# Moving the matmul row buffers of a two-part transformer to byte 64 modulo 512 of a partition

## The chip, the cores and the metric

The kernel runs on one core of a Trainium2 chip. Its time is the device time of one execution in microseconds (us); the figure used is the median of three runs. A core has five engines that run side by side and meet only at semaphores: TensorE (PE in the profile; its weight loads are shown apart as PEld), VectorE (DVE), ScalarE (ACT), GpSimd (POOL) and SyncE (SP), which here only issues weight DMAs. Tiles live in SBUF, 128 partitions wide; a "byte" of a buffer below is its start address inside each partition. Matmul results go to PSUM, which has eight banks.

## The reference, cut to what matters

Two transformer blocks in turn, each of two layers, on 256 rows of 1024 columns in float32. Every layer has a mixer and a gated feed-forward part, and almost all of the work is products of normalised rows with weights:

```python
for l in range(DEPTH):                       # first block
    h = rms_norm(x, g_mix[l])
    proj = h @ w_in[l]                       # 1024 x 10052: attention, convolutions, gates
    ...                                      # four branches, each @ a 512 x 1024 weight
    x = x + merged @ w_merge[l]
    h2 = rms_norm(x, g_ffn[l])
    gt = causal_dwconv(h2 @ w_ffn_gate[l], ffn_conv_w[l])
    x = x + (jax.nn.silu(gt) * (h2 @ w_ffn_up[l])) @ w_ffn_down[l]
...                                          # second block: layer 0 compressed and selected attention,
x = x + mix                                  # layer 1 dilated attention
x = x + swiglu(rmsnorm(x, norm_ffn[layer]), ffn_w_up[layer], ffn_w_down[layer])
```

## The kernel before

Each float32 operand of a product is split into a rounded high part and the remainder, both of type float32r, and a product is three passes: high by high, high by low, low by high (`three_passes`, lines 467 to 469). So every row buffer comes in two parts: `hT` (high and low, 2 x 8 x 256 columns in the tile `h_place`), `mixer_rows`, `ffn_rows`, `blocks_rows`, `dilated_rows` (the raw, turned rows before their norm is known, made in `raw_T`, line 538), `query_rows`, `branch` and `hidden`. All except `hT` are placed over one large tile, `work`, at an element given by hand.

Weights come as a stream of 277 units, most of them 1024 rows by 256 columns (128 partitions by 2048 elements, 1 MiB). SP loads a unit into one of three raw slots (line 2738); it may do so when the remainder of the unit three before has been made. ScalarE makes the high part into one of four `whi` slots (`make_high`, L435); VectorE, or GpSimd for some units of the mixers, makes the remainder into one of three `wlo` slots (`make_low`, L443), which frees the raw slot. A unit is 48 passes on TensorE (24 with 512 columns). A matmul has a stationary operand, loaded first, and a moving one, streamed past it. Where the result is wanted turned, a piece of 128 weight columns is stationary and the rows move (`columns_product`); elsewhere 128 rows are stationary and the weights move. In the profile the names after the arrow stand in the order moving, stationary: `psum<-hT,whi` has hT moving.

The program is a row of stages, in each of which every engine runs a list written out by hand: setup; twice mixer, merge product, feed-forward up, feed-forward down; compressed attention, its output product, feed-forward up and down; dilated attention, output product, feed-forward up and down; final norm. The mixer takes 48 units, the first four from `mixer_rows`, all later ones that read rows from `hT` (as moving operand 26, as stationary 10, one of them narrow). `ffn_up_stage` (line 855) takes 22 units, gate and up in turn: the first four from `ffn_rows`, 18 from `hT`. Its loop over pairs c runs, on ScalarE: high part of the unit four ahead, SiLU (L905), high part of the next, high part of the result (L909); on VectorE: the gate's norm or copy, its short convolution in the first block (L946, L949), the low part of the result before (L969), the product (L963), then two remainders of weights (L443). `take_unit` (line 455) makes TensorE wait for the remainder of a unit.

Later the compressed attention reads `hT` as moving operand in 8 units and the dilated one in 3; `add_rows_product` takes `hT` as stationary operand against 512 weight columns.

Of the kernel before, what the change touches and what calls it, by code (L numbers as in the profile page):

```python
# [28 lines left out]
P = 128  # L29
D = 1024  # L30
S = 256
TT = S // P
KT = D // P
# [200 lines left out]
def two_part_transformer(nc, a, consts, onehots, out):  # L234
    ctx = ExitStack()
    with ctx:
        place = {}

        def sb(name, shape, dt=F32):
            place[name] = -(-nc.sbuf_base // 32) * 32  # L240
            return ctx.enter_context(nc.sbuf_tensor(name, shape, dt))
# [2 lines left out]
            return Signal(ctx.enter_context(nc.semaphore(name)))  # L244

        x = sb("x", [P, TT, D])
        h_place = sb("h_place", [P, 2 * KT * S])
        raw = sb("raw", [P, RAW_SLOTS, UNIT])
        whi = sb("whi", [P, HIGH_SLOTS, UNIT], F32R)
        wlo = sb("wlo", [P, LOW_SLOTS, UNIT], F32R)  # L250
# [14 lines left out]
        at_h, at_work = place["h_place"], place["work"]  # L265

        def over(name, base, start, shape, dt=F32R):

            return nc.alloc_sbuf_tensor_at(name, [P] + shape, dt, offset=base + 4 * start)

        hT_both = over("hT", at_h, 0, [2, KT, S])
        hT = [hT_both[:, i] for i in range(2)]

        ROWS = 32
# [261 lines left out]
            root_ready.close(n)  # L536

        raw_T = {}
        for kind, rows_at in (("mixer", 19088), ("ffn", 14400), ("blocks", 15456), ("dilated", 17920)):
            raw_T[kind] = [over(f"{kind}_rows{i}", at_work, rows_at + i * KT * S, [KT, S]) for i in range(2)]  # L540
        part_sum = stat[:, 152:156]
        root = stat[:, 4:4 + TT]
# [2264 lines left out]
```

How the kernel before makes its waits and increments, by code:

```python
        def begin(eng):  # L393
            if stage[0]:
                eng.wait_ge(stage_done.sem, COMPUTE * stage[0])
# [1 line left out]
        def end(eng):  # L397
            eng.drain().then_inc(stage_done.sem, 1)
# [10 lines left out]
        def v_wait(n):  # L409
            nc.vector.wait_ge(vector_step.sem, n)
# [9 lines left out]
        def s_wait(n):  # L420
            nc.scalar.wait_ge(scalar_step.sem, n)
# [6 lines left out]
        def make_high(act, upto):  # L428
            while stream.high < min(upto, len(stream.units)):
                n = stream.high
                act.wait_ge(raw_landed[n % RAW_SLOTS], 16 * (n // RAW_SLOTS + 1))
                if n >= HIGH_SLOTS:
                    act.wait_ge(*stream.freed[n - HIGH_SLOTS])
                act.activation(part(whi, n, HIGH_SLOTS), part(raw, n, RAW_SLOTS), ACT.Copy).then_inc(high_made, 1)
                stream.high += 1
# [1 line left out]
        def make_low(eng, n):  # L438
            eng.wait_ge(high_made, n + 1)
            if n >= LOW_SLOTS:
                eng.wait_ge(*stream.freed[n - LOW_SLOTS])
            eng.tensor_tensor(part(wlo, n, LOW_SLOTS), part(raw, n, RAW_SLOTS),
                              part(whi, n, HIGH_SLOTS).bitcast(F32), ALU.subtract).then_inc(stream.low[n][0], 1)
# [10 lines left out]
        def take_unit(pe, n):  # L455
            pe.wait_ge(*stream.low[n])
            _, kt, _, _ = stream.units[n]
            return [part(b, n, k).rearrange("p (k c) -> p k c", k=kt) for b, k in ((whi, HIGH_SLOTS), (wlo, LOW_SLOTS))]
# [18 lines left out]
        def await_pair(pe):  # L478
            if handed_over:
                pe.wait_ge(*handed_over.pop(0))
```

## Time and profile before

| | us |
|---|---|
| median of three runs | 1822.07 |
| the three runs | 1816.26, 1822.07, 1826.09 |
| span of the profiled execution, first to last instruction | 1816.4 |
| TensorE busy, matmul | 1761.0 (97%) |
| TensorE busy, weight loads | 1663.7 (92%) |
| VectorE busy | 1220.7 (67%) |
| ScalarE busy | 932.6 (51%) |
| GpSimd busy | 124.6 (7%) |
| chain that ended last: TensorE's share | 84% |

The span is what the profile gives of the profiled execution's own time; it lies inside the range of the three timed runs. TensorE takes a matmul before the one ahead has ended, so the duration of one is longer than the distance from start to start; both are used below, and they are named apart. The granted clock of TensorE is shown in tenths of 2.4 GHz, over 40 slices of the span; it has two levels, 2.4 and 1.2 GHz.

### The profile page before, as it was taken

To read this page: it belongs to the slowest core of one execution; us is meant where nothing else is said; L and a number is where in the kernel's file an instruction comes from. 1 tells how busy PE (TensorE), PEld (TensorE's weight loads), DVE (VectorE), ACT (ScalarE), POOL (GpSimd) and SP (SyncE) were. 2 spreads that over 40 slices of the span, in tenths; PEclk is the share of its full clock that TensorE was granted. 3 is DMA by queue.
4 is the path that set the end of the run, shared out by engine and by line. 5 is a ranking of instruction groups with operands and counts; after the bars stand their busy time and mean duration, and the time that the engine had idled before them with its cause. 6 is when DMAs were issued, how large, how long until landed. Compare 5 with 4: busy or idle time off the path is not lost.

```text
span 1816.4 us, 31727 instructions
## 1 busy us (share of the span) xinstructions
PE 1761.0 (97%) x13416; PEld 1663.7 (92%) x13416; DVE 1220.7 (67%) x1927; ACT 932.6 (51%) x1291; POOL 124.6 (7%) x35
## 2 busy tenths in 40 slices
PE   7999999999999999999999998889999999999998
PEld 6999999899989999999999898769998899889986
DVE  6984855787749877567877466977554655655553
ACT  5445655454435545664544355755443565654442
POOL 1620300000004603000000000000000000000000
PEclk9899999999999999999999999989999999999999
DMA  7684546445554544546455546314555476435551
GB/s 236 174 207 128 180 133 210 163 163 186 207 188 146 186 150 153 186 140 206 149 190 190 177 156 170 123 64 139 186 186 209 165 215 166 129 121 181 186 220 70
DMA packets 248637, 305.75 MB, mean 168 GB/s; under 512 B 9267, under 2 KB 223631, under 8 KB 248496
## 3 DMA queue, kind: packets, MB, share of 16 engines
q1 hardware_dynamic: 235959, 289.66, 48.6%
q10 hardware_dynamic: 12536, 14.06, 4.0%
q8 instruction: 106, 1.74, 0.4%
q14 instruction: 36, 0.29, 0.0%
HBM read 299.51 MB, written 4.19 MB: 167 GB/s over the span
## 4 chain that ended last, share of the span: by engine, by line
PE 84%; DVE 7%; DMA 4%; ACT 3%; issue 1%; DVEq 0%; POOL 0%; SPq 0%; ACTq 0%; POOLq 0%
PE psum L467 25%; PE psum L468 25%; PE psum L469 25%; DVE wlo L443 2%; DMA raw<-in_w_in 1%; DMA raw<-in_a_w_in 1%; PE psum L2477 1%; PE psum L2503 1%; DMA x<-in_x 1%; DMA raw<-in_b_w_q 1%; PE psum L2489 1%; ACT whi L435 0%; ACT work L2563 0%; DVE work L2292 0%; PE psum L1119 0%
## 5 line engine op out<-in xcount | busy, mean ns | idle before, releaser
L435 ACT ACTIVATE whi<-raw 128x2048 fp32r<-128x2048 f32 (+2 forms) x277 | 526.6, 1903 | 543.9 <-PE psum L469 183.5
L443 DVE TENSOR_TENSOR wlo<-raw,whi 128x2048 fp32r<-128x2048 f32 x249 | 563.4, 2281 | 191.8 <-PE psum L469 157.5
L467 PE MATMUL psum<-hT,whi 128*128 128x256 f32 x2160 | 615.4, 285 | 4.9 <-DVE wlo L443 2.5
L469 PE MATMUL psum<-hT,wlo 128*128 128x256 f32 x2160 | 612.4, 284 | 0.0
L468 PE MATMUL psum<-hT,whi 128*128 128x256 f32 x2160 | 612.3, 283 | 0.0
L467 PEld LDWEIGHTS psum<-hT,whi 128*128 128x128 f32 x2160 | 414.7, 192 | 6.2 <-DVE wlo L443 3.1
L468 PEld LDWEIGHTS psum<-hT,whi 128*128 128x128 f32 x2160 | 414.6, 192 | 0.2
L469 PEld LDWEIGHTS psum<-hT,wlo 128*128 128x128 f32 x2160 | 414.4, 192 | 0.0
L443 POOL TENSOR_TENSOR wlo<-raw,whi 128x2048 fp32r<-128x2048 f32 (+1 forms) x28 | 123.4, 4411 | 588.7 <-ACT whi L435 401.2
L467 PE MATMUL psum<-whi,hT 128*128 128x256 f32 (+2 forms) x448 | 143.7, 321 | 1.1 <-issue 0.8
L469 PE MATMUL psum<-whi,hT 128*128 128x256 f32 (+2 forms) x448 | 143.0, 319 | 0.0
L468 PE MATMUL psum<-wlo,hT 128*128 128x256 f32 (+2 forms) x448 | 143.0, 319 | 0.0
L467 PE MATMUL psum<-whi,hidden 128*128 128x512 f32 x352 | 138.1, 392 | 1.1 <-issue 1.1
L468 PE MATMUL psum<-wlo,hidden 128*128 128x512 f32 x352 | 138.0, 392 | 0.0
L469 PE MATMUL psum<-whi,hidden 128*128 128x512 f32 x352 | 137.5, 391 | 0.0
L963 DVE TENSOR_TENSOR work<-work,psum 128x512 f32<-128x512 f32 x44 | 30.2, 687 | 134.4 <-PE psum L469 63.0
L467 PEld LDWEIGHTS psum<-whi,hT 128*128 128x128 f32 x448 | 88.3, 197 | 8.2 <-issue 3.3
L1476 DVE SCALAR_TENSOR_TENSOR psum<-work,par,psum 128x256 f32<-128x256 f32 x240 | 94.7, 480 | 0.1
L469 PEld LDWEIGHTS psum<-whi,hT 128*128 128x128 f32 x448 | 88.4, 197 | 5.0
L468 PEld LDWEIGHTS psum<-wlo,hT 128*128 128x128 f32 x448 | 88.3, 197 | 4.9
L467 PEld LDWEIGHTS psum<-whi,hidden 128*128 128x128 f32 x352 | 66.1, 188 | 16.4 <-issue 1.8
L469 PEld LDWEIGHTS psum<-whi,hidden 128*128 128x128 f32 x352 | 66.1, 188 | 14.6
(361 smaller groups left out, 2792.6 us busy)
## 6 DMA issues: line engine op xcount, KB each, us to landing
raw<-in_w_in SPq DMA_DIRECT2D x78, 1024.0 KB, 5.3
raw<-in_ffn_w_up SPq DMA_DIRECT2D x44, 1024.0 KB, 5.2
raw<-in_w_ffn_gate SPq DMA_DIRECT2D x22, 1024.0 KB, 5.3
raw<-in_w_ffn_up SPq DMA_DIRECT2D x22, 1024.0 KB, 6.0
raw<-in_w_ffn_down SPq DMA_DIRECT2D x22, 1024.0 KB, 4.8
raw<-in_ffn_w_down SPq DMA_DIRECT2D x22, 1024.0 KB, 4.9
raw<-in_b_w_q SPq DMA_DIRECT2D x12, 1024.0 KB, 6.1
raw<-in_a_w_in SPq DMA_DIRECT2D x10, 1024.0 KB, 5.4
```

What stands on the lines that cost most here:

```text
L435: act.activation(part(whi, n, HIGH_SLOTS), part(raw, n, RAW_SLOTS), ACT.Copy).then_inc(high_made, 1)
L443: eng.tensor_tensor(part(wlo, n, LOW_SLOTS), part(raw, n, RAW_SLOTS), part(whi, n, HIGH_SLOTS).bitcast(F32), ALU.subtract).then_inc(stream ...
L467: nc.tensor.matmul(dst, left[0], right[0], start=first, stop=False)
L468: nc.tensor.matmul(dst, left[0], right[1], start=False, stop=False)
L469: return nc.tensor.matmul(dst, left[1], right[0], start=False, stop=last)
L963: v_link(dve.tensor_tensor(prod[:, c % 2], cacc[:, c % 2], u, ALU.mult))
L1476: ins = dve.scalar_tensor_tensor(acc, glu[:, ct, k:k + S], tap, acc, ALU.mult, ALU.add)
L2477: mm = nc.tensor.matmul(slot(e)[:, st * keys:(st + 1) * keys], d_q[j // 2 % 2][lo:lo + DH, st, j % 2, t * P:(t + 1) * P], d_k[lo:lo + DH, ...
L2489: mm = nc.tensor.transpose(turn_bank(s, m)[:, i * P:(i + 1) * P], probs[:, 2 * (s % 2) + e, n * P:(n + 1) * P], ident)
L2503: mm = nc.tensor.matmul(b[DH * e:DH * e + DH, t * P:(t + 1) * P], d_v[:, st, kt, g * DH:(g + 1) * DH], turned_probs[s % 2][:, 768 * e + n ...
```

## The change

`h_place` grows by 128 elements (512 bytes), and `hT` starts 112 elements (448 bytes) into it. Buffers behind it move by 512 bytes. The raw rows of the mixer move down by 16 elements in `work`, those of the feed-forward stages up by 64. Weight slots stay at byte 128 modulo 512. No instruction is added or taken away.

```diff
@@ -244,7 +244,9 @@
         x = sb("x", [P, TT, D])
-        h_place = sb("h_place", [P, 2 * KT * S])
+        PHASE = 512 // 4
+        LEAD_ROWS = PHASE - 16
+        h_place = sb("h_place", [P, 2 * KT * S + PHASE])
         raw = sb("raw", [P, RAW_SLOTS, UNIT])
@@ -268,7 +270,7 @@
-        hT_both = over("hT", at_h, 0, [2, KT, S])
+        hT_both = over("hT", at_h, LEAD_ROWS, [2, KT, S])
         hT = [hT_both[:, i] for i in range(2)]
@@ -536,7 +538,7 @@
         raw_T = {}
-        for kind, rows_at in (("mixer", 19088), ("ffn", 14400), ("blocks", 15456), ("dilated", 17920)):
+        for kind, rows_at in (("mixer", 19072), ("ffn", 14464), ("blocks", 15456), ("dilated", 17920)):
             raw_T[kind] = [over(f"{kind}_rows{i}", at_work, rows_at + i * KT * S, [KT, S]) for i in range(2)]
```

## Rows read from the trace of the kernel before

**Rows 1.** The page: TensorE's busy time; its busy tenths and granted clock in 40 slices.
```profile
PE 1761.0 (97%) x13416; PEld 1663.7 (92%) x13416; DVE 1220.7 (67%) x1927; ACT 932.6 (51%) x1291; POOL 124.6 (7%) x35
...
PE   7999999999999999999999998889999999999998
...
PEclk9899999999999999999999999989999999999999
```

**Rows 2.** Line 467 by operands: count; ns of one, min/median/max; first, last start.
```profile
L467 PE MATMUL psum<-hT,whi x2160: 277/283/775, 96.6 to 1746.3; 128*128 128x256 f32 x197
...
L467 PE MATMUL psum<-branch,whi x256: 276/276/367, 236.9 to 848.1; 128*128 128x256 f32 x128
...
L467 PE MATMUL psum<-ffn_rows,whi x192: 281/281/468, 363.3 to 1642.7; 128*128 128x256 f32 x192
...
L467 PE MATMUL psum<-query_rows,whi x192: 276/276/387, 1468.4 to 1571.6; 128*128 128x256 f32 x192
...
L467 PE MATMUL psum<-mixer_rows,whi x96: 280/283/468, 23.7 to 572.7; 128*128 128x256 f32 x96
...
L467 PE MATMUL psum<-whi,dilated_rows x32: 279/279/467, 1439.6 to 1450.8; 128*128 128x256 f32 x32
```

**Rows 3.** Timeline of TensorE, start and length in us: first, last pass of two units.
```profile
1278.23 0.28 PE L467 MATMUL psum<-hT,whi 128*128 128x256 f32 x1
...
1283.87 0.28 PE L469 MATMUL psum<-hT,wlo 128*128 128x256 f32 x1
...
321.87 0.28 PE L467 MATMUL psum<-branch,whi 128*128 128x256 f32 x1
...
327.19 0.28 PE L469 MATMUL psum<-branch,wlo 128*128 128x256 f32 x1
```

**Rows 4.** Groups of TensorE by line and form: busy us, mean ns; idle before.
```profile
L467 PE MATMUL psum<-whi,hidden 128*128 128x512 f32 x352 | 138.1, 392 | 1.1 <-issue 1.1
...
L467 PE MATMUL psum<-whi,hT 128*128 128x512 f32 x128 | 50.1, 392 | 1.1 <-issue 0.8 <-DVE hT L2352 0.3
```

**Rows 5.** VectorE and ScalarE in up stages, bracketed: idle before, releaser; last, total waits.
```profile
419.86 4.50 DVE L443 TENSOR_TENSOR wlo<-raw,whi 128x2048 fp32r<-128x2048 f32 x2 [0.32 <-DVE work L963]
...
427.66 1.92 ACT L435 ACTIVATE whi<-raw 128x2048 fp32r<-128x2048 f32 x1 [5.63 <-DMA raw<-in_w_ffn_gate]
...
430.19 0.69 DVE L963 TENSOR_TENSOR work<-work,psum 128x512 f32<-128x512 f32 x1 [2.04 <-ACT work L905]
431.19 4.49 DVE L443 TENSOR_TENSOR wlo<-raw,whi 128x2048 fp32r<-128x2048 f32 x2 [0.32 <-DVE work L963]
...
1312.99 0.69 DVE L963 TENSOR_TENSOR work<-work,psum 128x512 f32<-128x512 f32 x1 [4.96 <-PE psum L469]
...
DVE work L963 <- ACT work L905: 48.4, 20, 5.6
```

**Rows 6.** Last two remainders of the first and third up stage; TensorE's first pass.
```profile
476.89 4.50 DVE L443 TENSOR_TENSOR wlo<-raw,whi 128x2048 fp32r<-128x2048 f32 x2 [0.31 <-DVE work L963]
...
480.48 0.28 PE L467 MATMUL psum<-hT,whi 128*128 128x256 f32 x1
...
1360.08 4.49 DVE L443 TENSOR_TENSOR wlo<-raw,whi 128x2048 fp32r<-128x2048 f32 x2 [0.32 <-DVE work L963]
...
1364.63 0.28 PE L467 MATMUL psum<-hT,whi 128*128 128x256 f32 x1
```

**Rows 7.** Timeline in the two mixers: a wait of TensorE, and VectorE's top-k stretch.
```profile
138.10 3.78 PE L1119 MATMUL psum<-work,cst 128*128 128x256 f32 x8 [5.10 <-ACT work L1375]
...
691.39 1.22 DVE L1494 TENSOR_TENSOR branch<-work,branch 128x1024 fp32r<-128x1024 f32 x1 [10.86 <-ACT branch L1296]
...
725.71 2.29 DVE L443 TENSOR_TENSOR wlo<-raw,whi 128x2048 fp32r<-128x2048 f32 x1
...
728.43 0.28 PE L467 MATMUL psum<-hT,whi 128*128 128x256 f32 x1
```

## The prediction

> **What bounds the kernel now.** I read the page's engine table and slices first: TensorE is busy 97% of a span of 1816.4 us, and only a few slices show an 8 [rows 1]. So the reader should ask two things: what sets the distance of one matmul pass from the next, and whether whatever feeds TensorE could feed it faster. For the first I read the view of line 467 by operands, then single passes in the timeline. The first five rows there are the same instruction, 128 rows by 256 columns in the same type, with only the moving buffer different, and yet their medians fall into groups: 283 ns where the moving operand is hT or mixer_rows, 281 with ffn_rows, 276 with branch and query_rows [rows 2]. The starts say the same of throughput: 48 passes of one weight unit with hT moving start from 1278.23 to 1283.87, 47 steps of 120.0 ns; 48 with branch moving start from 321.87 to 327.19, 47 steps of 113.2 ns [rows 3]. Nothing waits inside either stretch.
>
> What parts the groups is the place of the buffer. The change says that weight slots start at byte 128 modulo 512 of a partition; everything between them and hT is a multiple of 512 bytes, so hT starts at 128 too. From mixer_rows' new place (64, at element 19072, 76288 bytes, a multiple of 512) the work area starts at 64. Then branch (element 4096), query_rows (13824) and dilated_rows (17920) start at 64, mixer_rows (19088) at 128, ffn_rows (14400) at 320. hT gets there by 448 bytes in front of it: 128 + 448 = 576, which is 64 modulo 512. Moving operand at 128, like the weights: 283, in two buffers far apart (hT lies ahead of the weight slots, mixer_rows near the end of the work area). Moving operand at 64: 276, in two other places. So a pass is dear when both operands begin at the same phase, and the change puts hT exactly where branch and query_rows are: 64 against 128.
>
> The Trainium skill, SBUF — State Buffer, "Who interferes with whom", says on the contrary that PE never waits on anyone, with separate read ports for the moving operand and the weight load. By it, no phase could matter, and the sum would be zero. The 6.8 ns between the rows, on one instruction, speak against it; it is kept as a rival.
>
> **The change part by part.** No instruction, wait or DMA is added or taken away; every edit is an address. The extra 512 bytes in h_place push all later buffers on by a whole 512, so their phases stay.
>
> Term 1, hT as moving operand: 2160 passes on each of three lines [rows 2], that is 135 units of 48. Each unit gets 48 x 6.8 ns = 0.327 us shorter. 26 units lie in each mixer, 18 in each of the four feed-forward stages, 8 in compressed attention, 3 in dilated: 8.5, 8.5, 4 x 5.9, 2.6, 1.0 us.
> Term 2, raw rows: mixer_rows goes 283 to 276, four units a layer, 1.3 us (in the first layer the first unit is held back by the loading of x, so 1.0). ffn_rows goes 281 to 276 [rows 2], 5 ns x 48 x 4 = 0.96 us a stage.
> Term 3, hT as stationary operand, 288 x 3 of the passes with 256 columns (nine units a mixer): the nearest row is dilated_rows, stationary at 64, with 279 against hT's 283 [rows 2]. Bounds: 0 and 4 ns each, 3.5 us in all; I take the middle, 1.7, since an overlapped pass may give back less than its duration. With 512 columns a pass takes 392 with hT at 128 and 392 with hidden at 64 [rows 4]: nothing.
> ScalarE and VectorE write hT and the rows at new places with the instructions that they have now; none of these writes stands in the feed-forward loop below, and I take 0 for them.
>
> TensorE's own saving is thus 10.4 (first mixer: 8.5 + 1.0 + 0.9), 10.7 (second), 4 x 6.9, 2.6 and 1.0: 52 us. It is not what the run gains, because of what is late next.
>
> Feed-forward up stages: here is a loop in which TensorE has no part. VectorE's subtraction for weights (L443) frees a raw slot, the next weight DMA goes into it, ScalarE rounds it (L435) when it has landed (idle 5.63 us, ended by that DMA), then does the SiLU (L905), VectorE's product waits for that (2.04 us idle, ended by ACT L905), and only behind this product stand the next two subtractions in VectorE's order. From one pair of subtractions to the next it is 419.86 to 431.19: 11.33 us for two units [rows 5]. TensorE needs 11.52 now (two times 48 passes of 120) and would need 10.87. So a pair gains at most 0.19 here, not 0.65. The product waited for ACT 20 times [rows 5]. Beyond that a stage can only use up the lead that the weights have by its end: the pair of subtractions starting at 1360.08 has its first part done 2.29 later, at 1362.37, and TensorE takes that unit at 1364.63: 2.26 us of lead, found alike in the second, third and fourth stage; in the first it is 480.48 - 479.18 = 1.30 [rows 6]. The gain of a stage is its lead plus the last unit's own 0.33: 1.6, 2.6, 2.6, 2.6. In the third the product still waits for TensorE [rows 5], about six pairs, so add 6 x 0.19 = 1.1. Sum 10.5 of 27.4.
>
> The Trainium skill, SBUF — State Buffer, "The DMA setup-cost knee", fits a DMA as 2 us plus bytes over 436 GB/s, an estimate of 4.4 us for a unit of 1 MiB. By it the loop would be about 10.2 us, below TensorE's 10.87, and the feed-forward stages would keep their whole 27.4. The rows differ: from 422.15, where the first subtraction ends, to 427.66, where ScalarE starts on what has landed [rows 5], it is 5.5 us.
>
> Mixers: in the first layer TensorE already waits 5.10 us for ScalarE at 138.10 [rows 7]; the seven units with hT moving before it save 2.3 us, of which this wait takes back between nothing and all. I take all, since ScalarE and not TensorE is late there. In the second layer VectorE works from 691.39 without a wait on TensorE (top-k) to its subtraction at 725.71 + 2.29 = 728.00, and TensorE takes that unit at 728.43, a lead of 0.43 [rows 7]. The five units before it save 1.6, so 1.2 is lost at the least; with what TensorE had gained before that chain began perhaps 2.5; I take 2.0. Left: 8.1 and 8.7.
> Compressed attention: its slices show TensorE at 8 [rows 1], it waits for others between the units; bounds 0 and 2.6, I take the middle, 1.3. Dilated: three units back to back, 1.0.
>
> Sum: 8.1 + 8.7 + 10.5 + 1.3 + 1.0 = 29.6 us. Against the profiled span that is 1816.4 - 29.6 = 1786.8. The span lies within 0.2 us of the fastest of the three runs (1816.26) and 5.7 under their median, so I take the difference off the median: 1822.07 - 29.6 = 1792.5.
>
> **The rivals.**
> Nothing happens: phase is not the cause (something else of the four buffers is), or the change doesn't bring hT where it says. By the skill's rule that PE never waits this is also the outcome. hT stays at 120 ns and the time near 1822. Against it: two buffers at 128 and two at 64, each pair alike to the nanosecond [rows 2]. For it: no buffer in hT's own stretch of addresses has been seen at 64.
> The loop gives way: were the landing shorter, TensorE would be the bound everywhere in the feed-forward stages; 29.6 + 16.9 = 46.5, 1775.5. Against: the product waits for ACT already now [rows 5].
> Half: the interval falls only to ffn_rows' group, 2 ns. TensorE saves about 13 us, some 10 of it kept: 1812.
> Slower: TensorE takes units sooner, weight transfers are packed closer and land later. Place: the four loops, 36 pairs. Price: each microsecond of landing adds one to a pair's 11.33. From 11.52 on the stage is slower than before; to undo the 19 us of the other stages, 36 pairs have to lose 0.53 each: a loop of 12.05, a landing 0.7 us later than in the row. At 1.1 later it is 36 x 0.91 - 19 = +14, 1836. Against: in that loop transfers are started by VectorE's subtractions, whose rhythm can change by 0.19 us only.
> That the clock falls through more idle time is not priced apart: the granted clock is 1.0 (a 9 in the slices) in all feed-forward stages, its upper level of 2.4 GHz, and fell to an 8 in two slices of 40 [rows 1]; the loop leaves TensorE 10.87 of 11.33, 96%.
>
> **How the numbers follow.** Forecast 1792.5: 0.82. Nothing: 0.06. Loop gives way: 0.05. Half: 0.04. Slower: 0.03. The range: mixers and compressed attention together leave 4 us to either side, loops another 4 up or 6 down by how transfers land, and the median of runs spread by 10 us may sit 4 off; I take 1782 to 1806, which leaves out all four rivals. A difference of under 0.5%, about 9 us, can't be told from no change here: faster takes the forecast, the loop's rival and most of the half, 0.90; same 0.07; slower 0.03.
>
> **What would show it.** Line 467's median with hT moving at 276 and steps of 113 ns; mixer_rows and ffn_rows at 276; hT stationary at about 279; the first two feed-forward stages hardly shorter, with TensorE waiting for L443 and pairs 11.3 apart; the VectorE chain of the second mixer now ahead of a TensorE wait of some 1.5 us. Wrong if hT stays at 283, if feed-forward stages shrink by 6 us each, or if pairs stand over 11.5 apart.

## The result and the profile after

The changed kernel takes 1810.85 us in the median (1808.78 to 1812.33) beside 1822.21 us of the kernel before in the same runs: a ratio of 0.9947, 95% interval 0.9929 to 0.9965. That is 0.5% faster, some 10 us (the two medians lie 11.4 us apart), where 29.6 were forecast, and outside the range of 1782 to 1806. The profiled execution has a span of 1810.5 us against 1816.4, 5.9 less. All lines of the code stand two further down than before: 469 to 471 are the three passes, 445 the subtraction, 437 the rounding, 907 the SiLU, 965 the product.

First the page of the kernel after: busy time, granted clock in 40 slices, and the shares of the chain that ended last.

```profile
PE 1741.8 (96%) x13416; PEld 1638.3 (90%) x13416; DVE 1226.3 (68%) x1927; ACT 933.3 (52%) x1291; POOL 125.9 (7%) x35
...
PEclk9899999999999999999999989999999999999999
...
PE 59%; DVE 21%; DMA 8%; ACT 5%; issue 5%; DVEq 1%; ACTq 0%; SPq 0%
```

TensorE is about as busy and as well clocked as before [rows 1], but only 59% of the last chain is its own, 84% before, and VectorE and DMA have 29%. Next line 469 of the kernel after by operands (count; ns of one, min/median/max; first and last start), the rows that answer to [rows 2].

```profile
L469 PE MATMUL psum<-hT,whi x2160: 276/281/775, 95.2 to 1740.5; 128*128 128x256 f32 x197
...
L469 PE MATMUL psum<-branch,whi x256: 276/281/366, 232.8 to 842.0; 128*128 128x256 f32 x128
...
L469 PE MATMUL psum<-ffn_rows,whi x192: 281/281/468, 359.1 to 1636.6; 128*128 128x256 f32 x192
...
L469 PE MATMUL psum<-query_rows,whi x192: 276/277/384, 1461.7 to 1565.5; 128*128 128x256 f32 x192
...
L469 PE MATMUL psum<-mixer_rows,whi x96: 276/281/468, 24.0 to 567.9; 128*128 128x256 f32 x96
```

The reader should look at the branch row first. Its buffers kept their phase, and its median rose from 276 to 281. hT fell from 283 to 281 and not to 276; but its minimum is 276 now. So the row mixes two kinds of passes. The timeline of TensorE (start, length in us) parts them: first and last pass of two weight units, as in [rows 3].

```profile
100.70 0.28 PE L469 MATMUL psum<-hT,whi 128*128 128x256 f32 x1
...
106.02 0.28 PE L471 MATMUL psum<-hT,wlo 128*128 128x256 f32 x1
...
1273.58 0.28 PE L469 MATMUL psum<-hT,whi 128*128 128x256 f32 x1
...
1279.11 0.28 PE L471 MATMUL psum<-hT,wlo 128*128 128x256 f32 x1
```

47 steps take 5.32 us in the first unit, 113.2 ns each, and 5.53 us in the second, 117.7 ns. Same buffer, same place, no wait in either. Going through all starts, nearly every unit is of one kind or the other, and the kind goes on from unit to unit as long as TensorE does not pause (a pause, here and below, is idle time of TensorE or a few passes of another form between two units): the stretch that holds 1273.58 starts at 1245.4 and has 1007 passes at 117.8 ns. Of 87 unbroken stretches of twelve passes or more over buffers at byte 64, 56 are at 113.3 ns and 31 at 117.8. Below, "fast" means 113.3, "middle" 117.8 and "slow" 120.0 ns from start to start; in a pass's own length they show as 276, 281 and 283 ns.

Then the first feed-forward loop of the kernel after, VectorE, ScalarE and TensorE (in brackets the idle time before and what ended it), and, for the whole execution, TensorE's waits for VectorE's subtraction (total, number, longest).

```profile
380.94 4.49 DVE L445 TENSOR_TENSOR wlo<-raw,whi 128x2048 fp32r<-128x2048 f32 x2 [0.32 <-DVE work L965]
...
427.57 4.49 DVE L445 TENSOR_TENSOR wlo<-raw,whi 128x2048 fp32r<-128x2048 f32 x2 [0.32 <-DVE work L965]
...
436.29 1.92 ACT L437 ACTIVATE whi<-raw 128x2048 fp32r<-128x2048 f32 x1 [7.02 <-DMA raw<-in_w_ffn_gate]
...
438.82 0.69 DVE L965 TENSOR_TENSOR work<-work,psum 128x512 f32<-128x512 f32 x1 [2.97 <-ACT work L907]
439.83 4.49 DVE L445 TENSOR_TENSOR wlo<-raw,whi 128x2048 fp32r<-128x2048 f32 x2 [0.32 <-DVE work L965]
...
442.17 0.39 PE L469 MATMUL psum<-hT,whi 128*128 128x256 f32 x1 [1.09 <-DVE wlo L445]
...
473.52 4.49 DVE L445 TENSOR_TENSOR wlo<-raw,whi 128x2048 fp32r<-128x2048 f32 x2 [0.32 <-DVE work L965]
...
PE psum L469 <- DVE wlo L445: 14.2, 18, 1.9
```

Pairs of subtractions are 11.57 us apart on average here (380.94 to 473.52, eight pairs). One of them, 427.57 to 439.83, is 12.26: a weight unit landed late, ScalarE idled 7.02 us for it, and TensorE waited 1.09. The kernel before had such late pairs too, here one of 12.45 us, in its own timeline:

```profile
384.94 4.49 DVE L443 TENSOR_TENSOR wlo<-raw,whi 128x2048 fp32r<-128x2048 f32 x2 [0.32 <-DVE work L963]
...
397.39 4.49 DVE L443 TENSOR_TENSOR wlo<-raw,whi 128x2048 fp32r<-128x2048 f32 x2 [0.31 <-DVE work L963]
```

From 384.94 to 476.89 [rows 6] it is 91.95 us for eight pairs, 11.49 each, not the 11.33 of the one pair that the prediction took [rows 5]. But in its whole execution TensorE waited for this subtraction 4 times and 4.5 us in all, against 18 times and 14.2 us now.

### The profile page after: what moved, and what is told of

It is laid out like the page before. It is cut to its first block, busy times and chain, and to the rows that moved or that the text cites. A ratio compares the mean times of both kernels' runs of the same rounds, so it can differ in the third digit from the quotient of the medians.

```text
span 1810.5 us, 31727 instructions
## 1 busy us (share of the span) xinstructions
PE 1741.8 (96%) x13416; PEld 1638.3 (90%) x13416; DVE 1226.3 (68%) x1927; ACT 933.3 (52%) x1291; POOL 125.9 (7%) x35
## 4 chain that ended last, share of the span: by engine, by line
PE 59%; DVE 21%; DMA 8%; ACT 5%; issue 5%; DVEq 1%; ACTq 0%; SPq 0%
PE psum L469 18%; PE psum L471 17%; PE psum L470 17%; DVE wlo L445 7%; DMA raw<-in_w_ffn_gate 4%; DVE psum L1478 3%; DMA raw<-in_w_in 1%; ACT whi L437 1%; DMA raw<-in_w_ffn_down 1%; DVE work L965 1%; DVE work L1610 1%; PE psum L2479 1%; DMA work<-in_a_w_v 1%; PE psum L2505 1%; DVE work L1608 1%
## 5 line engine op out<-in xcount | busy, mean ns | idle before, releaser
L445 DVE TENSOR_TENSOR wlo<-raw,whi 128x2048 fp32r<-128x2048 f32 x249 | 563.6, 2282 | 182.9 <-PE psum L471 146.0
L469 PE MATMUL psum<-hT,whi 128*128 128x256 f32 x2160 | 608.2, 282 | 13.6 <-DVE wlo L445 11.7
L470 PE MATMUL psum<-hT,whi 128*128 128x256 f32 x2160 | 602.5, 279 | 0.0
L471 PE MATMUL psum<-hT,wlo 128*128 128x256 f32 x2160 | 602.3, 279 | 0.0
L469 PEld LDWEIGHTS psum<-hT,whi 128*128 128x128 f32 x2160 | 409.6, 190 | 18.8 <-DVE wlo L445 16.3
L470 PEld LDWEIGHTS psum<-hT,whi 128*128 128x128 f32 x2160 | 407.4, 189 | 0.2
L471 PEld LDWEIGHTS psum<-hT,wlo 128*128 128x128 f32 x2160 | 407.1, 188 | 0.0
L445 POOL TENSOR_TENSOR wlo<-raw,whi 128x2048 fp32r<-128x2048 f32 (+1 forms) x28 | 124.6, 4455 | 580.7 <-ACT whi L437 404.7
```

Source lines behind the costliest of these rows:

```text
L445: eng.tensor_tensor(part(wlo, n, LOW_SLOTS), part(raw, n, RAW_SLOTS), part(whi, n, HIGH_SLOTS).bitcast(F32), ALU.subtract).then_inc(stream ...
L469: nc.tensor.matmul(dst, left[0], right[0], start=first, stop=False)
L470: nc.tensor.matmul(dst, left[0], right[1], start=False, stop=False)
L471: return nc.tensor.matmul(dst, left[1], right[0], start=False, stop=last)
```

## The experiments

In the profiles named below each unit's kind is read from the starts of its passes, as above. "Turned", "fast" and so on always mean that.

**Is it the shift of all other buffers?** The pad stays, hT and the raw rows go back to their phases of before.

```diff
-        LEAD_ROWS = PHASE - 16
+        LEAD_ROWS = 0
-        (("mixer", 19072), ("ffn", 14464), ...)
+        (("mixer", 19088), ("ffn", 14400), ...)
```

> The pad of 512 bytes stays, so every buffer behind it lies 512 bytes higher, as in the changed kernel; hT goes back to byte 128 modulo 512, mixer rows to byte 128 and feed-forward rows to byte 320, as before the change. Theory A (a run of passes without a pause takes its interval at its start and keeps it; byte 128 gives 120 ns, other phases 113.3 or 117.8 ns): hT at 120.0 ns start to start, branch and query units all at 113.3 as before, because they follow 120 ns passes or the same pauses as before; time as before, 1816 to 1826 us. Theory B (the shift by 512 bytes itself took 113 from the branch and query units): hT 120, but branch and query units partly at 117.8, as in the changed kernel, so 13 or so units lose 0.21 us each: 1822 to 1827 us.

Measured: 1816.57 us, ratio 0.9993 (0.9976 to 1.0009). Line 469 of this kernel by operands:

```profile
L469 PE MATMUL psum<-hT,whi x2160: 277/283/562, 98.1 to 1743.5; 128*128 128x256 f32 x197
...
L469 PE MATMUL psum<-branch,whi x256: 276/276/367, 231.2 to 844.6; 128*128 128x256 f32 x128
```

hT is slow, all 16 branch units are fast again: the shift itself does nothing, theory B falls. Two of the twelve query units were middle here (as in e7 below, which has no shift), and some feed-forward rows at byte 320 were fast, which in the kernel before were all middle. So A's second half, that branch and query come out fast because they did before, holds only for runs that follow slow passes.

**Which phases have which intervals?** Only LEAD_ROWS changes, to 64, 32, 16, 120 and 48.

```diff
-        LEAD_ROWS = PHASE - 16
+        LEAD_ROWS = 64
```

> hT alone moves on, to byte 384 modulo 512 (half a period from the weight slots); mixer and feed-forward rows stay at byte 64 as in the changed kernel. Theory A (drawn at the start of a run, phase only says which values can be drawn): hT runs at a mix of 113.3 and 117.8 ns, time 1800 to 1815 us. Theory C (each phase has one interval of its own and the changed kernel's mix comes from something else, such as the pauses): one interval for every hT run, either 113.3 (1788 to 1797 us) or 117.8 (1808 to 1816 us).

> As the run with byte 384, with hT at byte 256 modulo 512. Theory A: a mix of 113.3 and 117.8 ns, 1800 to 1815 us. Theory C: one interval for all hT runs, 1788 to 1797 us at 113.3, 1808 to 1816 us at 117.8, 1822 us at 120.

> As the run with byte 384, with hT at byte 192 modulo 512, as far above the weight slots' byte 128 as the changed kernel's byte 64 lies below it. Theory A: a mix of 113.3 and 117.8 ns, 1800 to 1815 us; the order of who collides with whom may turn round, so the share of 113.3 may differ from the half seen at byte 64. Theory C: one interval for all hT runs.

> hT at byte 96 modulo 512, 32 bytes nearer to the weight slots' byte 128 than in the changed kernel, all else as in it. Theory A: a mix of two or three values per run; if what counts is which of the 64-byte steps the first byte lies in, as at byte 64; if it counts to the byte, something between byte 64 (115.6 ns on average) and byte 128 (120 ns). 1808 to 1818 us.

> hT at byte 320 modulo 512, all else as in the changed kernel. If the phases repeat every 256 bytes (bytes 128 and 384 both gave 120 ns throughout), it behaves as byte 64 did: 113.3 and 117.8 ns in about equal parts, 1806 to 1814 us. If the period is 512: other values, 117.8 ns throughout as the feed-forward rows at byte 320 showed in the kernel before, 1810 to 1816 us.

Measured, with the mean distance of successive passes over hT inside the units (weights at byte 128, or 640 for the second half of a unit's columns; both are 128 modulo 512):

| hT at byte (modulo 512) | ns, start to start | kinds of unbroken stretches | us, ratio to before |
|---|---|---|---|
| 128 (kernel before) | 120.0 | all slow | 1 |
| 384 | 120.0 | all slow | 1817.97, 1.0004 (0.9987 to 1.0022) |
| 256 | 118.8 | 118.6 to 118.8 in 115 of 133 whole units, slow in 18 | 1814.42, 0.9987 (0.9968 to 1.0006) |
| 96 | 118.3 | 118.3 or so in every whole unit, none fast | 1820.0, one execution |
| 192 | 117.2 | 45 middle, 6 fast | 1812.71, 0.9979 (0.9959 to 0.9999) |
| 320 | 115.9 | 29 middle, 31 fast | 1810.36, one execution |
| 64 (the change) | 115.6 | mixed | 1810.85, 0.9947 (0.9929 to 0.9965) |

At byte 384 the feed-forward and mixer rows still lie at byte 64, so this run is also the raw rows' part of the change alone: no gain that can be measured. Its row is that of the kernel before:

```profile
L469 PE MATMUL psum<-hT,whi x2160: 277/283/775, 96.0 to 1746.1; 128*128 128x256 f32 x197
```

Both theories missed there, A expected a mix and C 113.3 or 117.8. Bytes 128 and 384 behave alike, and so do 64 and 320: in these two pairs the pattern repeats after 256 bytes, not 512. C falls by the mixes at 64, 192 and 320, where A holds, with the addition that a phase sets which kinds are open and how often each comes up. At 96 and 256 neither theory had the values right: byte 96 has one value of its own, as C would have it, but neither 113.3 nor 117.8, and the time was above what was expected. First and last pass of a unit there:

```profile
1275.36 0.28 PE L469 MATMUL psum<-hT,whi 128*128 128x256 f32 x1
...
1280.92 0.28 PE L471 MATMUL psum<-hT,wlo 128*128 128x256 f32 x1
```

That is 47 steps of 118.3 ns. No phase tried has fast stretches alone, and byte 64 is as good as any.

**Is the draw the program's?** The changed kernel, profiled in another execution.

> The changed kernel once more, to see whether a run of passes takes the same interval in another execution. Theory A1 (the interval is drawn at the start of a run and hangs on the timing of that start): some runs of the same unit that were at 113.3 ns are at 117.8 now or the reverse; runs that follow the same waits keep their value mostly. Theory A2 (the draw is fixed by the program): every unit as in the first profile. Time 1808 to 1813 us beside 1818 to 1822 us of the kernel before.

Measured: 1810.59 us, ratio 0.9951 (0.9928 to 0.9974). The same weight unit (the 26th, with hT moving) in the two profiles, line 469 in the window of that unit, the first profile and this one:

```profile
L469 PE MATMUL psum<-hT,whi x17: 281/281/281, 183.3 to 189.0; 128*128 128x256 f32 x17
```

```profile
L469 PE MATMUL psum<-hT,whi x16: 276/276/276, 188.7 to 193.8; 128*128 128x256 f32 x16
```

The first eighteen units agree, then the two profiles part; stretches behind like waits are often alike, not always. A1 holds: the interval is not a property of the program, and a placing gives a share of fast units.

**Can a stretch be made to draw again?** Narrow extra passes in the 1007-pass stretch of the third feed-forward loop.

```diff
+            if nudge:
+                nc.tensor.matmul(b[:, 0:nudge], w[0][:, 0, 0:P], src[0][:, 0, 0:nudge], start=True, stop=True)
```

> The changed kernel with 16 extra passes in the third feed-forward loop alone (a run of 1007 passes at 117.8 ns without a pause): ahead of units 6 to 21 of that loop one pass of 64, 64, 128, 128, 192, 192, 32, 32, 96, 96, 160, 160, 224, 224, 16 and 16 columns with the unit's own operands, whose result the unit's first pass overwrites. Each costs 0.11 us or so, 1.8 us in all. Theory A (the interval is taken at the start and held, and any pass of another length is a new start): the interval stays constant between the extra passes and changes only at them; at least one unit of the 16 runs at 113.3 ns. Rival B (the interval belongs to the unit, its slots or the stage): all of them stay at 117.8 ns. Time 1809 to 1813 us with all at 117.8, 0.2 us less for each unit at 113.3.

Measured: 1811.16 us. TensorE's timeline around one of them (line 489 is the extra pass, here of 128 columns), from the second pass of the unit ahead to the last of the unit behind:

```profile
1277.44 0.28 PE L470 MATMUL psum<-hT,whi 128*128 128x256 f32 x1
...
1282.86 0.28 PE L471 MATMUL psum<-hT,wlo 128*128 128x256 f32 x1
1282.98 0.22 PE L489 MATMUL psum<-hT,whi 128*128 128x128 f32 x1
...
1283.21 0.28 PE L470 MATMUL psum<-hT,whi 128*128 128x256 f32 x1
...
1288.45 0.28 PE L471 MATMUL psum<-hT,wlo 128*128 128x256 f32 x1
```

46 steps are 5.42 us ahead of it (117.8 ns each) and 5.24 behind (113.9, the run-in included). In this execution the stretch began fast and turned middle at the first extra pass. Of the sixteen units behind an extra pass five were fast, and each kept its kind to the next extra pass; the six behind 16, 32 and 64 columns were middle, three of them after a fast unit. A holds, B falls.

**What withholds TensorE's gain in the feed-forward loops?** ScalarE's order in that loop, in the changed kernel and in the kernel before.

```diff
-                    make_high(act, n0 + 2 * c + 5)
                     silu(c)
+                    make_high(act, n0 + 2 * c + 5)
```

> The changed kernel with one order changed: in the feed-forward loop ScalarE does the SiLU of a pair ahead of the rounding of the next gate unit, instead of behind it. Theory R (the loop closes through a ring: first low part 2.25 us, landing of the next gate unit 5.5, its rounding 1.92, SiLU 0.61, product 0.69 and 0.31 to the next low part, together 11.3 us a pair): without SiLU and product in it the ring is about 9.7 us, TensorE's two units bind, 10.9 us at 113.3 ns and 11.3 us at 117.8 ns, TensorE's waits for L445 inside the loops go (11.7 us in the changed kernel, most of them there), and the time falls by 3 to 9 us to 1801 to 1808 us. Rival: the landings alone bind the loop: pairs stay at 11.2 to 11.4 us and the time at 1808 to 1813 us.

> The kernel before with the same change of order on ScalarE and nothing else. Theory R: with hT at 120 ns a pair takes TensorE 11.52 us, more than the ring's 11.3, so taking SiLU out of the ring gives nothing but the single waits of some pairs: 0 to 2 us off, within the scatter of the kernel before. Rival: the order itself is worth the same with either placing, 3 to 9 us.

Measured: on the changed kernel 1795.87 us, ratio 0.9891 (0.9855 to 0.9926), below what was expected; on the kernel before 1817.83, ratio 0.9999 (0.9982 to 1.0016). The first loop of the changed kernel with the new order, VectorE, ScalarE and TensorE's waits:

```profile
411.14 0.69 DVE L965 TENSOR_TENSOR work<-work,psum 128x512 f32<-128x512 f32 x1 [1.56 <-PE psum L471]
412.15 4.50 DVE L445 TENSOR_TENSOR wlo<-raw,whi 128x2048 fp32r<-128x2048 f32 x2 [0.32 <-DVE work L965]
...
423.03 4.49 DVE L445 TENSOR_TENSOR wlo<-raw,whi 128x2048 fp32r<-128x2048 f32 x2 [0.32 <-DVE work L965]
...
408.92 0.64 ACT L907 ACTIVATE work<-work 128x512 f32<-128x512 f32 x1 [4.58 <-DVEq L955]
PE psum L469 <- DVE wlo L445: 6.0, 5, 1.9
```

The pairs are 10.88 us apart, which is TensorE's own two units at 113.3 ns, the product waits for TensorE and no longer for the SiLU, and TensorE's 18 waits for L445 have become 5. On the kernel before the pairs are 11.52 apart, TensorE's two units at 120:

```profile
414.28 4.49 DVE L443 TENSOR_TENSOR wlo<-raw,whi 128x2048 fp32r<-128x2048 f32 x2 [0.32 <-DVE work L963]
...
425.80 4.50 DVE L443 TENSOR_TENSOR wlo<-raw,whi 128x2048 fp32r<-128x2048 f32 x2 [0.32 <-DVE work L963]
```

Theory R holds in both: the ring was there before too and cost next to nothing, since TensorE was nearly as slow; with the shorter passes it is the bound.

**Can the fast kind be had at will?** Two extra passes of the slow kind (both operands in the weight slot at byte 128) ahead of long stretches, with either order of ScalarE.

```diff
+        def collide(b, w):
+            for _ in range(2):
+                nc.tensor.matmul(b[:, 0:S], w[0][:, 0, 0:P], w[0][:, 0, 0:S], start=True, stop=True)
...
+                    if n == 5:
+                        collide(bank(first_bank(n)), w)
```

> The run with SiLU ahead of the rounding, and in it, ahead of nine long runs of passes, two extra passes of 256 columns whose two operands both lie at byte 128 modulo 512 (0.24 us each time, their result is overwritten): unit 5 of each feed-forward loop, units 15, 24 and 40 of both mixers, the first hT unit of the dilated layer (11 places, 2.6 us in all). Theory A with a rule for the draw (a run that follows 120 ns passes without a pause comes out at 113.3 ns, as it did 20 times of 20 in the five kernels with hT at 120): all these runs at 113.3 ns; beside the run without extra passes the third feed-forward loop gains 3.6 us, mixers 4 to 6, the dilated layer 1.3, less 2.6: 1786 to 1793 us. Rival (the draw stays open after the two passes): a mix as before and the cost of the passes, 1796 to 1800 us.

> The changed kernel with the same extra passes ahead of the same nine kinds of runs and nothing else (SiLU stays behind the rounding). Theory A with the rule: those runs at 113.3 ns until their first pause. Theory R (the ring of 11.2 to 11.3 us a pair withholds what TensorE saves in the first, second and fourth feed-forward loop): only the third loop, the mixers and the dilated layer gain, 9 to 11 us less 2.6: 1801 to 1806 us, and the rest of the way to the run with SiLU ahead is the ring's. Rival (the intervals alone kept the changed kernel from its forecast): 1790 to 1796 us.

> The run with SiLU ahead of the rounding and two extra passes at 120 ns, with those passes moved one unit on where a pause of TensorE came just ahead of them: unit 6 instead of 5 of each feed-forward loop, units 16 and 41 instead of 15 and 40 of the mixers; unit 24 and the dilated layer's first hT unit stay. Theory A with the rule (120 ns passes in a running stream are always followed by 113.3 ns): all eleven runs at 113.3 ns in every execution, so the first feed-forward loop (16 units at 117.8 in the profile of the run before, 3.4 us), units 41 to 47 (1.5 us) and the second and third of the runs at 15 (0.8 us) come on top: 1786 to 1791 us, with less scatter. Rival (it is the unit's place, not the pause): the runs at 16 and 41 stay mixed, 1792 to 1797 us.

> The same with two extra passes more ahead of unit 2 of each feed-forward loop (three units of 0.21 us each gained if they come out at 113.3 ns, less 0.24) and ahead of unit 7 of both mixers, where hT is the stationary operand and the weights move. Theory A with the rule at every placing: 1784 to 1790 us. Rival (the rule holds for the order whi stationary, hT moving alone, and the runs at unit 7 stay at 117.8 ns): 1786 to 1791 us, no better than the run without them.

Measured, as ratios: e9 0.9862 (0.9828 to 0.9895), 1794.3 us; e10, which keeps the SiLU behind, 0.9935 (0.9909 to 0.9962), 1807.2; e13 0.9862 (0.9833 to 0.9890), 1795.1; e14 0.9901 (0.9876 to 0.9926), 1800.4. In e9 and e10 the ten stretches without a pause ahead all came out fast, of the twelve behind a pause (four behind idle time, eight behind passes of another form) five. Moving the passes behind the pause, in e13, should then have given eleven fast stretches; it gave six, and four of the five others had been fast ahead of the extra passes. That is the point: in a running stream two slow passes turn the kind over. In e13 and e14 together 17 of 18 middle stretches with hT or rows moving became fast and 8 of 8 fast ones became middle; the two with hT stationary stayed middle. The rule of the expectations falls, the turning takes its place; the times of e9, e13 and e14 also came out above what that rule gave. For the loops, e10 answers the other question: its third loop and the mixers' long stretches were mostly fast, and yet it is 12.9 us slower than e9, which ran beside it and differs from it by ScalarE's order alone. So the intervals alone did not keep the changed kernel from its forecast.

**How many slow passes until the past is forgotten, and does turning pay?** One to eight slow passes ahead of the units of the third loop of the changed kernel (the cut below; COUNTS names how many for each unit); and the new order with two slow passes ahead of unit 2 of each loop, beside the new order alone.

```diff
+                    if counted and n in COUNTS:
+                        collide(bank(first_bank(n)), w, COUNTS[n])
```

> The changed kernel with extra passes at 120 ns ahead of units 6 to 21 of the third feed-forward loop: one, one, one, two, two, two, three, three, three, four, four, four and four times eight of them. Theory A with turning: after two passes the interval changes over each time; after eight the stream has reached its 120 ns rhythm and the next unit is at 113.3 ns whatever went before, all four times. Rival (an even count turns, however long): the four units behind eight passes alternate between 117.8 and 113.3 ns. The passes cost 7.4 us in all: 1812 to 1820 us.

> The run with SiLU ahead of the rounding, with two extra passes at 120 ns ahead of unit 2 of each feed-forward loop and nowhere else. Unit 1 of these loops ran at 117.8 ns in 27 of 32 loops of the profiles with hT and rows at byte 64. Theory A with turning (two such passes in a running stream turn 117.8 ns into 113.3 ns and the reverse): units 2 to 4 of the loops that start so, and units 5 to 21 of the loops without a pause, come out at 113.3 ns; the third loop gains 20 units of 0.21 us, 4.2, less 0.24, the others 0.4 each, so 3 to 5 us less than the run without extra passes beside it. Rival (the turning was chance): 0 to 1 us more than that run.

> The run with SiLU ahead of the rounding of the next gate unit once more, beside the other two: 1793 to 1799 us as before, a ratio of 0.986 to 0.992 to the kernel before; the share of units at 113.3 ns differs from the first profile, since the value of a run is drawn anew in each execution.

Measured in e16 (1813.2 us), TensorE's timeline in the third loop; line 489 is the extra passes, the rows between them are first and last pass of a unit:

```profile
1285.42 0.39 PE L489 MATMUL psum<-whi 128*128 128x256 f32 x2
1285.65 0.28 PE L469 MATMUL psum<-hT,whi 128*128 128x256 f32 x1
...
1291.19 0.28 PE L471 MATMUL psum<-hT,wlo 128*128 128x256 f32 x1
1291.31 0.40 PE L489 MATMUL psum<-whi 128*128 128x256 f32 x2
1291.54 0.28 PE L469 MATMUL psum<-hT,whi 128*128 128x256 f32 x1
...
1296.88 0.28 PE L471 MATMUL psum<-hT,wlo 128*128 128x256 f32 x1
...
1339.67 0.29 PE L469 MATMUL psum<-hT,whi 128*128 128x256 f32 x1
...
1345.02 0.28 PE L471 MATMUL psum<-hT,wlo 128*128 128x256 f32 x1
1345.13 1.10 PE L489 MATMUL psum<-whi 128*128 128x256 f32 x8
1346.08 0.29 PE L469 MATMUL psum<-hT,whi 128*128 128x256 f32 x1
...
1351.42 0.28 PE L471 MATMUL psum<-hT,wlo 128*128 128x256 f32 x1
```

47 steps take 5.54, then 5.34 us: two slow passes turned a middle unit into a fast one. Behind eight passes it is 5.35 and 5.34: fast behind fast, which two or four had turned each time. All four units behind eight passes were fast, three after a fast unit and one after a middle one; one pass kept fast fast three times, three passes gave both. Theory A with turning holds. In e15 units 2 to 21 of all four loops were fast, as expected, but the time, 1798.0 us (0.9884, 0.9853 to 0.9914), isn't below that of the order alone beside it, 1796.69 (0.9868, 0.9841 to 0.9894): by time alone the rival's "0 to 1 us more" came nearer, and the 3 to 5 us expected can't be told in executions that scatter by 6 to 9. The version to keep is the change with SiLU ahead: 0.9891 and 0.9868 in two comparisons, against 0.9947 and 0.9951 for the change.

Time of twenty units in each feed-forward stage, from the first pass over hT to the first pass of the third unit of the product behind it, in us, read from the starts in each profile, tells the two effects apart:

| kernel | first | second | third | fourth |
|---|---|---|---|---|
| before | 117.3 | 116.4 | 115.2 | 115.2 |
| before, SiLU ahead | 116.4 | 116.4 | 115.2 | 115.3 |
| after | 117.1 | 115.6 | 113.3 | 115.4 |
| after, other execution | 117.5 | 116.9 | 113.3 | 113.9 |
| after, two slow passes (e10) | 117.6 | 116.8 | 111.3 | 113.3 |
| after, SiLU ahead (e6) | 111.1 | 111.0 | 113.3 | 109.4 |
| after, SiLU ahead, other execution (e17) | 111.1 | 111.6 | 113.3 | 113.2 |
| after, SiLU ahead, two slow passes (e9) | 115.0 | 111.4 | 109.9 | 109.9 |
| after, SiLU ahead, turned (e15) | 111.1 | 111.4 | 109.4 | 109.4 |

Without the new order the first two stages take 115.6 to 117.6 in these profiles whatever the passes do. With it, a stage whose hT units are all or nearly all fast takes 109.4 to 111.6, a middle one 113.2 to 115.0. The first stage parts the two effects best: 15 of its 18 hT units were fast in the kernel after and 17 in e6, and it took 117.1 and 111.1.

## Why the prediction missed

The direction was right, and so was the cause: the phase of hT against the weight slots sets the distance of passes, and moving it off byte 128 ends the 120 ns. That it is the two operands' bytes together, and not the moving one's own, is seen where the weights are what moves, at byte 128 in both kernels: with hT stationary at 128 all 18 whole units are at 120.0, with it at 64 all 18 at 113.3 or 117.8. Two steps of the sum failed.

**The step "moving operand at 64: 276".** It read a phase as a value, from branch and query_rows [rows 2, 3]. In the kernel before, all five stretches over branch or query rows that began without a pause followed slow passes over hT, and behind these the stretch was fast 20 times of 20 in the four kernels with hT slow. The stretches behind a pause were fast 14 times of 14 in that profile and 12 of 14 in each of the three others, so luck had its part in the others. The change took the slow passes away, and branch became a mix itself (median 281). Term 1, 44.1 us, was mis-sized: the mean step fell from 120.0 to 115.6 ns, not to 113.2, which is 6480 x 4.4 = 28.5 us. Branch and query lost 768 x 3.2 and 576 x 1.7 ns, 3.4 us, which the sum did not have. Term 2 gave 384 x 4.1 and 768 x 0.8 ns, 2.2 instead of 6.1; term 3 gave 864 x 3.5 ns, 3.0 against 1.7 taken and 3.5 as its upper bound. TensorE's own saving by the distance of passes was thus 30 us, not 52. (Its busy time on the page fell by less, from 1761.0 to 1741.8, and its idle time rose by 13.3; the first step behind a pause is 0.2 to 0.3 us long, and pauses became more, but the difference was not followed to its end.) A sign of it was in the trace before: dilated_rows, at byte 64 against weights at 128, which the prediction read by its length of 279 alone. First and last pass of a unit of the kernel before:

```profile
1445.45 0.28 PE L467 MATMUL psum<-whi,dilated_rows 128*128 128x256 f32 x1
...
1450.99 0.28 PE L469 MATMUL psum<-whi,dilated_rows 128*128 128x256 f32 x1
```

That is 47 steps of 117.8 ns, and so are its two other whole units: byte 64 did not mean 113 even then.

**The step "the gain of a stage is its lead plus the last unit's own 0.33".** Predicted for the four feed-forward stages 1.6, 2.6, 3.7 and 2.6 us, 10.5; between the two profiles it is 0.2, 0.8, 1.9 and -0.2, 2.7. The mechanism was the right one, e6 and e7 show it: DMA, rounding, SiLU, product, subtraction close a ring. Its size was off: 11.33 us was one pair; with the late pairs of 12.3 to 12.5 the mean of the first loop was 11.49 before and 11.57 after, as long as TensorE's 11.52. Pairs over 11.5 apart were one of the prediction's own signs of being wrong. In the second stage, without such late pairs, the lead was drawn on, but eight pairs took 90.8 us where they had taken 90.1, and the ring goes on for one pair beyond the loop's last unit, into the product, which the sum left out:

```profile
985.59 4.50 DVE L445 TENSOR_TENSOR wlo<-raw,whi 128x2048 fp32r<-128x2048 f32 x2 [0.31 <-DVE work L965]
...
997.90 4.49 DVE L445 TENSOR_TENSOR wlo<-raw,whi 128x2048 fp32r<-128x2048 f32 x2 [0.32 <-DVE work L965]
...
1000.24 0.50 PE L469 MATMUL psum<-whi,hidden 128*128 128x512 f32 x1 [0.58 <-DVE wlo L445]
```

The last unit's remainder was done at 985.59 + 2.29 = 987.88 and TensorE took it at 988.03, with 0.15 us of lead left of 2.26. The stage was then 1.6 us ahead, and the product's second unit, waiting for the pair of 997.90, gave half of that back. In the fourth stage two late pairs took 13.65 and 12.92 us, 12.41 and 12.37 before; in the other execution of the changed kernel it was 12.31 and 12.22, and the stage gained 1.3. Why these weights land late was not tested. The third stage alone was TensorE's, and there 18 units at 117.8 ns gained 18 x 0.11 = 1.9, as the starts have it.

**Mixers, 16.8 predicted.** The second gained 1.7 us between the profiles instead of 8.7. Of its 26 units over hT 10 were fast; six of its eight branch units lost 0.21 us each; the narrow unit and the one behind it took back 1.5 and a wait 1.3. This wait is the one that was foretold at 1.5 us, TensorE behind VectorE's top-k chain [rows 7], and so that step held. The wait of the first mixer grew from 5.10 to 5.62; TensorE's timeline after:

```profile
722.68 0.39 PE L469 MATMUL psum<-hT,whi 128*128 128x256 f32 x1 [1.47 <-DVE wlo L445]
...
136.04 3.78 PE L1121 MATMUL psum<-work,cst 128*128 128x256 f32 x8 [5.62 <-ACT work L1377]
```

The wait of the first mixer thus took back 0.5 us, where the sum took 2.3 (six units with hT moving lie ahead of it, not seven), and TensorE was through it 2.06 us earlier than before, at 136.04: ScalarE's release came earlier too. In the first mixer as a whole 4.6 came out, but profiles of one and the same change differ there by as much (313.8 and 318.7 us), and the kernel with hT slow and a mere shift had 312.7: nothing can be told of it. Compressed attention lost 2.3 where 1.3 were expected, in a stretch that took 154 to 161 us in the other profiles; that too stays open. The dilated layer lost 0.3: its hT units were middle, and seven of twelve query units fast where all had been.

**The rivals.** "Half", 1812 us at a chance of 0.04, came nearest in time, and its mechanism, that the step falls only to that of ffn_rows, is what the middle stretches are. It should have had the larger share: one buffer at 320, off the weights' phase, stood at 281 all along. "Nothing happens" is out: hT's steps went from 120.0 to 115.6 ns in the mean. The Trainium skill, SBUF — State Buffer, "Who interferes with whom", has TensorE's two read ports independent; here steps of 113, 118 and 120 ns by the addresses of the two operands disagree with it. "The loop gives way" didn't come by itself, and came with the order of ScalarE. "Slower" did not come as a result. Late landings that a faster TensorE feels are what the 1.09 us wait at 442.17 shows; that they come later because TensorE takes units sooner, as that rival had it, is not shown, since in the first loop the kernel before had pairs as late (12.45 and 12.29 us beside 12.42 and 12.26).

## What to carry to other kernels

A median by operand is a mixture until the minimum and the start-to-start distances say otherwise; and a rate that a buffer shows belongs to its predecessor in the stream too, so it can't be carried to another buffer from its address alone. When an engine's work gets shorter, measure a loop beside it over all its turns, not over one, and ask at once what closes the ring; here one exchange of two ScalarE instructions, worth nothing before, was worth about as much as the change itself or more (0.9947 became 0.9891 and 0.9868).

## What the runs showed of the hardware

A stream of passes of 256 columns with a weight load each keeps a steady rhythm that hangs on the start bytes of its two operands, at the same granted clock of 1.0 (2.4 GHz) in both units shown first. With moving operand and weights at the same byte modulo 256, 120.0 ns was seen throughout. At 64 or 192 bytes beside it 113.3 and 117.8 are both steady, and a stream keeps the one that it started with, over 1007 passes in the longest case, until a pause or a pass of another kind. With hT at byte 96 it was 118.3, at 256 mostly 118.6 to 118.8. With rows or hT moving at byte 64 two passes at the same phase turned one rhythm into the other (17 of 18 and 8 of 8 times in e13 and e14), a longer stretch of them ended in 113.3 (20 of 20 behind hT's slow passes, 4 of 4 behind eight), and the same program draws differently from execution to execution. What inside the chip makes these rhythms was not tested.
